# One more block pair by seven products in the first pair of output columns, and the matrix-LSTM's stage and y's sums in other slots

## The reference

```python
h = rms_norm(x, norm_g[l])
proj = jnp.einsum('bsd,dn->bsn', h, w_in[l])
...
y = jnp.concatenate([y_a, y_b, y_c], axis=-1)
x = x + jnp.einsum('bsm,md->bsd', y, w_out[l])
```

## Time and profile before

| | us |
|---|---|
| median of 3 runs (1515.27 to 1516.86) | 1515.87 |
| profiled execution, its own time | 1517.49 |
| span of its instructions | 1515.7 |
| PE busy in the span | 1511.2 |
| DVE busy | 1138.1 |
| ACT busy | 813.0 |
| POOL busy | 360.2 |

### The profile page before, as it was taken

One profiled execution on the slowest core, in us unless ns is written; L12 is line 12 of the kernel. 1 busy time (PEld: TensorE's weight loads), 2 busy tenths in 40 slices (PEclk: granted clock), 3 DMA queues, 4 the chain that ended last, 5 costly groups with the idle time before them and its releaser, 6 DMA issues.

```text
span 1515.7 us, 19030 instructions
## 1 busy us (share of the span) xinstructions
PE 1511.2 (100%) x6906; PEld 1251.9 (83%) x6906; DVE 1138.1 (75%) x1714; ACT 813.0 (54%) x1084; POOL 360.2 (24%) x606
## 2 busy tenths in 40 slices
PE   9999999999999999999999999999999999999999
PEld 7888888888888887888878888888888888888887
DVE  6889899757759855576579676676557779988885
ACT  6766656587533444554545545544345645555553
POOL 9040131330230040126520254344400112000000
DMA  9887687986788785558865787898875667686766
GB/s 292 279 237 220 198 248 205 233 250 195 223 247 263 242 221 165 159 183 267 254 201 167 231 250 199 246 276 235 250 244 174 189 214 235 195 237 207 220 214 163
DMA packets 207438, 338.32 MB, mean 223 GB/s; under 512 B 53065, under 2 KB 60536, under 8 KB 207088
## 3 DMA queue, kind: packets, MB, share of 16 engines
q1 hardware_dynamic: 184784, 288.66, 62.5%
q0 software_dynamic: 22512, 48.42, 12.1%
q10 hardware_dynamic: 48, 0.02, 0.0%
HBM read 312.81 MB, written 27.68 MB: 225 GB/s over the span
## 4 chain that ended last, share of the span: by engine, by line
PE 94%; DVE 4%; DMA 1%; ACT 1%; issue 1%; ACTq 0%; DVEq 0%
PE acc L1275 25%; PE acc L1278 25%; PE acc L1277 25%; PE mix L1275 2%; PE mix L1278 2%; PE mix L1277 2%; PE mix L1293 1%; PE mix L1291 1%; PE mix L1292 1%; PE acc L1291 1%; PE acc L1293 1%; PE acc L1292 1%; DVE w_lo L1994 1%; PE mix L1384 1%; PE mix L1467 1%
## 5 line engine op out<-in xcount | busy, mean ns | idle before, releaser
L1994 DVE TENSOR_TENSOR w_lo<-w_raw,w_hi 128x1024 fp32r<-128x1024 f32 (+1 forms) x505 | 606.8, 1215 | 251.2 <-ACT w_hi L1612 245.7
L1612 ACT ACTIVATE w_hi<-w_raw 128x1024 fp32r<-128x1024 f32 (+1 forms) x505 | 525.6, 1050 | 388.6 <-PE acc L1278 284.1
L1275 PE MATMUL acc<-w_hi,op_hi 128*128 128x512 f32 (+1 forms) x1636 | 644.0, 394 | 0.3 <-DVE w_lo L1994 0.3
L1278 PE MATMUL acc<-w_hi,op_lo 128*128 128x512 f32 (+1 forms) x1636 | 637.1, 389 | 0.0
L1277 PE MATMUL acc<-w_lo,op_hi 128*128 128x512 f32 (+1 forms) x1636 | 637.0, 389 | 0.0
L1275 PEld LDWEIGHTS acc<-w_hi,op_hi 128*128 128x128 f32 x1636 | 307.5, 188 | 64.8 <-issue 1.3
L1278 PEld LDWEIGHTS acc<-w_hi,op_lo 128*128 128x128 f32 x1636 | 307.3, 188 | 64.2
L1277 PEld LDWEIGHTS acc<-w_lo,op_hi 128*128 128x128 f32 x1636 | 307.5, 188 | 61.7
L979 POOL DMA_DIRECT2D conv_dram<-y x48 | 30.7, 699 | 166.6 <-DVE y L2086 119.5
L1275 PE MATMUL mix<-w_hi,op_hi 128*128 128x512 f32 x162 | 62.9, 388 | 0.0
L1277 PE MATMUL mix<-w_lo,op_hi 128*128 128x512 f32 x162 | 62.9, 388 | 0.0
(11 more groups left out here) (558 smaller groups left out, 1761.9 us busy)
## 6 DMA issues: line engine op xcount, KB each, us to landing
w_raw<-in_w_in_dram SPq DMA_DIRECT2D x367, 512.0 KB, 4.6
w_raw<-in_w_out_dram SPq DMA_DIRECT2D x128, 512.0 KB, 4.4
w_raw<-in_w_in_dram SPq DMA_DIRECT2D x16, 384.0 KB, 3.8
w_raw<-in_a_wuq_dram SPq DMA_DIRECT2D x12, 512.0 KB, 5.4
out_dram<-in_x_dram POOLq DMA_DIRECT2D x7, 512.0 KB, 6.8
conv_dram<-y POOLq DMA_DIRECT2D x48, 64.0 KB, 4.0
y<-conv_dram POOLq DMA_DIRECT2D x48, 64.0 KB, 4.4
w_raw<-in_a_wuqi_dram SPq DMA_DIRECT2D x6, 512.0 KB, 4.4
```

What stands on the lines that cost most here:

```text
L1275: nc.tensor.matmul(o, hi[:, kt, tok], hv[:, i, n0:n1], start=(kt == (kts if late else blk["kts"])[0]), stop=False)
L1278: last_mm = nc.tensor.matmul(o, lo[:, kt, tok], hv[:, i, n0:n1], start=False, stop=(kt == blk["kts"][-1]))
L1612: func(split_ap(w_hi, c), w_raw[:, c % RAW_BUFS, 0:n], ACT.Copy).then_inc(hi_ready, 1)
L1994: vec.tensor_tensor(split_ap(w_lo, c), w_raw[:, c % RAW_BUFS, 0:n], split_ap(w_hi, c).bitcast(F32), ALU.subtract).then_inc(lo_ready, 1)
```

## The change

The first pair of output columns (p=2) takes a sixth row group, i=13, by seven products; its row groups come in another order. Positions in the list count pairs of chunks from chunk 432. In the new list seven-product groups stand at chunks 438, 442, 448, 452, 456 and 460 (before: 442, 446, 452, 456 and 460).

```diff
-PAIR_KTS = [[4, 5, 6, 7, 15, 8, 14, 9, 13, 0, 10, 1, 11, 2, 12, 3], [15, 4, 8, 5, 6, 9, 7, 10, 14, 11, 0, 12, 1, 13, 2, 3],
+PAIR_KTS = [[4, 5, 6, 8, 7, 9, 15, 14, 10, 0, 11, 1, 12, 2, 13, 3], [15, 4, 8, 5, 6, 9, 7, 10, 14, 11, 0, 12, 1, 13, 2, 3],
             [15, 8, 4, 9, 5, 10, 6, 11, 7, 12, 0, 13, 1, 14, 2, 3]]
 SEVEN = [[0, 1, 2, 3, 4, 5], [0, 1, 2, 3, 4, 5],
-         [8, 9, 10, 11, 12], [8, 9, 10, 11, 12, 13], [8, 9, 10, 11, 12, 13, 14]]
+         [8, 9, 10, 11, 12, 13], [8, 9, 10, 11, 12, 13], [8, 9, 10, 11, 12, 13, 14]]
...
-S_PIECES = [(0, 10, 12), (10, 18, 19), (23, 29, 32), (23, 29, 37), (26, 35, 37), (35, 36, 40), (45, 49, 51)]
-A_SLOTS = [(4, 6, 9), (12, 15, 25), (23, 27, 32), (30, 34, 44)]
-YD_SLOTS = [34, 40, 55, 61]
+S_PIECES = [(3, 20, 22), (3, 23, 25), (27, 30, 31), (29, 32, 33), (38, 41, 46), (40, 49, 50), (54, 64, 68)]
+A_SLOTS = [(2, 4, 7), (10, 12, 25), (16, 26, 31), (28, 34, 39)]
+YD_SLOTS = [33, 42, 50, 64]
```

## The result

The changed kernel takes 1521.13 us in the median of 6 runs (1519.37 to 1522.78), the kernel before 1515.99 in 6 runs beside them: a ratio of 1.0033, 95% interval 1.0022 to 1.0043. It is slower by 5.1 us. The forecast was 1517.7 with no change that can be told, its range ended at 1520.1: that the sum is a loss was right, its size was not. The profiled execution took 1520.95 us, with a span of 1519.2.

A forecast was written before the change was run, and what follows sets the result against it. PE's own work was taken to bound the kernel: 1517.49 - 0.68 (product) + 2.35 (wait at chunk 430) + 0.2 (chunk 443) = 1519.4 us, in terms of the runs' median 1517.7 us. The range was 1515.0 to 1520.1.

The forecast's parts named there:

- The product saved: Row group 13 goes from 24 to 21 matmuls: 0.68 us less on PE.
- DVE's and ACT's costs: Row group 13's sums and splits: 4.4 us more on DVE, some 1.6 us more on ACT, which has room.
- y's sums moved: Pieces sl 8 to sl 13 each still stand ahead of their use; the moves were priced at nothing.
- Steps 1, 2 and 5: Before chunk 430: ap 2 starts 2.32 us earlier, block 30's evacuation 3.2 later; yd 0 to chunk 430 takes 8.2.
- Steps 3 and 4: y's first block lands 19.9 us after add_out(0), at 1230.8; yd 0, moved ahead of ap 3, holds DVE till then.
- The landing from which a wait was to begin, 1228.5: If y's first block lands no later than 1228.5, PE has no wait at chunk 430.
- The prediction's own rule, a microsecond for a microsecond: At chunk 430, a landing one microsecond later makes PE's wait one microsecond longer.
- Afterwards: Behind chunk 430 DVE has no lead left; PE waits 0.2 us at chunk 443, nothing to 1.5 us.
- The rival of a lead that isn't won back: More PE waits at chunks 439, 443 and 456, 1520.1 us; decides from 3.7 us of waits; chance 0.25.
- The rival of a turn as quick as the second block's: y's first block returns from HBM in 17.1 us, only the product counts: 1515.2 us; chance 0.18.

The follow-up runs named there:

- e4: Changed kernel's slots, but the first pair has five seven-product groups in the order of before: 1522.6 us, 1.0040 of the kernel before.
- e9: Kernel before with only the sixth seven-product group and the new row-group order, all slots as before: 1518.06 us, ratio 1.0011.
- e10: Changed kernel with ap 2 back in slot 419 and yd 0 in slot 428, behind ap 3: 1515.68 us, 0.9995 of the kernel before.
- e5: Kernel before with ap 2 in slot 418 and yd 0 in slot 425, nothing else: 1522.16 us, ratio 1.0037.
- e6: Kernel before with yd 0 in slot 425 alone: 1516.21 us, ratio 0.9999.
- e7: Kernel before with ap 2 in slot 418 alone: 1516.15 us, ratio 1.0000.
- e2: Changed kernel with ap 2 back in slot 419, yd 0 still in 425: 1515.79 us, 0.9997 of the kernel before.
- e3: Changed kernel with ae 3 back in slot 422 instead of 420: 1520.93 us, 1.0030 of the kernel before.
- e12: Changed kernel with ap 2 back in slot 419 and add_out(0) made to wait for chunk 423's rounding: 1521.92 us, 1.0038 of the kernel before.
- e1: Changed kernel with yd 0 in slot 430 instead of 425: 1516.69 us, 0.9999 of the kernel before.
- e11: Changed kernel with the turn of y's first block ahead of add_out(0) in POOL's queue: 1516.17 us, 0.9995 of the kernel before.
- e8: Changed kernel with yd 0 in slot 430 and 8.7 us of unused DVE work in slot 425: 1521.16 us, 1.0036 of the kernel before.

## Why the prediction was wrong

*The product saved, DVE's and ACT's costs, y's sums moved.* Right in what they mean for PE: 6903 matmuls, 4.1 us more on DVE (4.4 forecast), no wait at any sl. ACT has 0.4 us more by its busy time, where 1.6 was forecast; it had room for either. e4, e9 and e10 fit the 0.68 us, which no single comparison here resolves.

*Steps 1, 2 and 5.* Right to 0.1 us in the evacuation, add_out(0) and the 8.2 us from yd 0 to chunk 430. That both the delayed turn and the moved yd 0 are needed is what e5, e6 and e7 show. The landing from which a wait was to begin, 1228.5, isn't contradicted by e2: yd 0 at 1226.45 there, 1227.7 in the clock of the kernel before (add 1.26, evacuations at 1204.60 and 1205.86), and no wait.

*Steps 3 and 4: the landing.* This is the term that failed first. I took 19.9 us behind add_out(0), on the ground that the same block stood behind the same transfer in the same queue. From add_out(0) to yd 0's start it was 22.0. The last packet came 21.6 us behind add_out(0), 1.8 later than the 19.8 of the kernel before (my 19.9 read the end of a window, 1227.6, for the last packet), and 0.4 went by from the last packet to yd 0's start, which I had left out because yd 0 found its block there before. DVE stood idle for 7.55 us ahead of yd 0, where some 5 were forecast. The prediction's own rule, a microsecond for a microsecond, gives 1232.88 + 8.2 - 1236.71 = 4.4 us; 4.28 and 0.1 were measured. It holds in e3, e4, e5 and e12 as well: from the start of yd 0, put into the clock of the kernel before, it gives 4.4, 3.9, 4.3 and 4.7 us, and PE's starts show 4.5, 3.9, 4.3 and 4.7. So the mechanism was right, and the duration of the transfers was the term that was too small. Its upper price, one microsecond more for 3.4, was too small a step: I had bounded the duration from the quicker side by a row (17.1) and from the slower one by nothing but a guess. The wait at chunk 429 is part of the same sum, since w_lo of 429 is ready 1.8 us behind the landing.

*The clock.* The second term, and one that I had not at all: 1.6 us behind the wait. The prediction says that any new wait of PE is added to the end in full, and leaves it at that; here the matmuls behind the wait ran at the lower clock for a while, so a wait cost more than its length. The late landing alone would have made some 1519.7 us, within the range; with the 1.6 it is 1521.3. It also helps to explain why e4, e5 and e12, with some 4 to 4.7 us of waits, come out 5.8 to 6 us slower.

*Afterwards.* 0.2 forecast; PE has no further wait in the changed kernel, and e1 shows the 0.2 at chunk 443 where PE doesn't stop before it. The rival of a lead that isn't won back named 3.7 us of waits as its point; the waits passed it, but at chunks 429 and 430 and not behind them, so that rival's mechanism did not happen.

*The rival of a turn as quick as the second block's* holds only for e11, where add_out(0) no longer stands ahead and the stores start earlier: from the first store to the last packet of POOL's queue at most 17.4 us.

## What to carry to other kernels

An engine that takes its work strictly in order should meet a piece that waits for a transfer behind the work that others need, not ahead of it: one slot was worth 6 us here (e7 against e5), and nothing where the transfer came earlier (e6). When a transfer is moved in time, its duration need not be that of the row before: started a few microseconds later, the same block took up to 2 us longer here. So price it with a bound above as well as below. And to a wait of the engine that sets the time, add what its clock may cost behind the wait.

## What the runs showed of the hardware

In the profile of the changed kernel TensorE's clock fell when PE was already busy again: the granted clock was 1.00 through the wait of 3.5 us, and 0.53 from 1.5 us behind its end, for 3.5 us. It does not happen in each execution. e12's stretches show it too:

```profile
1240.00:1241.00 1.00, 0.96 (x4) 0.82 (x5) 1.00 (x3) 1.00 (x2) 0.00 (x0) 1.00 0.00 0
1241.00:1244.00 3.00, 3.00 (x9) 2.35 (x8) 3.00 (x3) 1.08 (x2) 0.00 (x0) 0.50 0.79 221
```

In e4's profile the granted clock was 1.00 for 1.3 us behind the wait and then 0.51 for 3.5 us. In e5's it was 0.50 from the first matmul behind the wait, for some 3 us. In e3's, with a wait of the same length, the starts stay 0.227 apart. Of the changed kernel's six runs the two with a mean granted clock of 1.000 took 1519.4 and 1520.2 us, the four below it 1521.0 to 1522.8. In e8 the three runs at 1.000 took 1520.4 to 1521.2, the two at 0.999 1523.2 and 1523.4. So beside its length such a wait cost nothing in some executions and about 2 us in others; what decides between them isn't shown here. The Trainium skill (TensorE: Matmul & The Clock Gate, "HAM oscillation — how this bites in real kernels") describes a kernel whose TensorE waits for data and starts its next work at the lower clock. e5's rows agree with that; in the changed kernel, e4 and e12 the first 1.0 to 1.5 us behind the wait were still at 1.00.
